# Regrouped projection steps and an rwkv stage that opens with its pair products

## The reference

```
def rwkv7_branch(p, mu, w0, w_up, a0, a_up, g_up, k_k, k_a, r_k, gn_g, gn_b):   # first block
    p = p + (token_shift(p) - p) * mu
    r, k, v, wd, ad, gd = _split(p, (A_WIDTH, A_WIDTH, A_WIDTH, A_RANK_W, A_RANK_A, A_RANK_G))
    w_log = -jax.nn.softplus(-(w0 + jnp.tanh(wd) @ w_up).astype(F32)) - 0.5
    decay = jnp.exp(-jnp.exp(w_log))
    a = jax.nn.sigmoid((a0 + ad @ a_up).astype(F32))
    g = jax.nn.sigmoid(gd) @ g_up
    kk = hd(k * k_k)
    kk = kk * lax.rsqrt(jnp.maximum(jnp.sum(kk * kk, axis=-1, keepdims=True), 1e-24))
    k_mod = hd(k.astype(F32) * (1.0 + (a - 1.0) * k_a.astype(F32)))
    y = rwkv7_scan(r_h, hd(decay), k_mod, v_h, -kk, kk * a_h)
    ...
def chunk_gated_delta_rule(q, k, v, g, beta):                                    # second block
    m = jnp.where(strict, jnp.einsum('bnhid,bnhjd->bnhij', k_beta, k) * decay_mat, 0.0)
    t_inv = lax.linalg.triangular_solve(eye + m, jnp.broadcast_to(eye, m.shape),
                                        left_side=True, lower=True, unit_diagonal=True)
    ...
```

## Time and profile before

| | |
|---|---|
| timed runs, median | 3095.12 us (3090.31 to 3096.48) |
| the profiled execution | 3103.75 us, its span 3100.7 us |
| mean granted TensorE clock | 0.925 |
| PE busy | 2743.8 us, 88% |
| DVE busy | 1880.1 us, 61% |
| ACT busy | 1342.8 us, 43% |
| DMA queue of the weights | 34.7% of 16 engines |

### The profile page before, as it was taken

How to read it: one execution, slowest core, us unless ns; L and a number is a source line. 1 busy time by engine, 2 the same in 40 slices (tenths; PEclk the granted TensorE clock), 3 DMA queues, 4 the chain that set the end, 5 groups by cost and what they waited for, 6 DMA issues and landing times. The chain is left out here.

```text
span 3100.7 us, 58400 instructions
## 1 busy us (share of the span) xinstructions
PE 2743.8 (88%) x25404; PEld 2336.9 (75%) x25404; DVE 1880.1 (61%) x2644; ACT 1342.8 (43%) x1882; POOL 87.9 (3%) x120
## 2 busy tenths in 40 slices
PE   7887778999887688999998888889999988978899
PEld 6776656888776657898887775678888877757788
DVE  5755766975765766956656444656565655446564
ACT  5413334655413244645453232544454532325453
POOL 0020000000110000000000200000000011000000
PEclk9897889999997889999998888989999988889999
DMA  5211114564211123554542121335655421113353
GB/s 222 96 43 55 69 56 149 192 214 174 83 59 52 69 96 136 203 196 165 203 152 103 42 71 40 112 138 201 221 179 203 151 77 56 69 41 130 143 199 128
DMA packets 54686, 386.48 MB, mean 125 GB/s; under 512 B 6688, under 2 KB 7328, under 8 KB 8352
## 3 DMA queue, kind: packets, MB, share of 16 engines
q1 hardware_dynamic: 54432, 382.76, 34.7%
HBM read 381.69 MB, written 1.05 MB: 123 GB/s over the span
## 5 line engine op out<-in xcount | busy, mean ns | idle before, releaser
L321 PE MATMUL banks<-normed_high,weights_high 128*128 128x256 f16 (+1 forms) x4096 | 1141.6, 279 | 42.7 <-DVE weights_low L307 20.1
L322 PE MATMUL banks<-normed_low,weights_high 128*128 128x256 f16 (+1 forms) x4096 | 1140.2, 278 | 0.0
L323 PE MATMUL banks<-normed_high,weights_low 128*128 128x256 f16 (+1 forms) x4096 | 1139.7, 278 | 0.0
L307 DVE SCALAR_TENSOR_TENSOR weights_low<-weight_ring,weights_high 128x2048 f16<-128x2048 f32 x334 | 761.2, 2279 | 406.3 <-ACT weights_high L301 391.9
L301 ACT ACTIVATE weights_high<-weight_ring 128x2048 f16<-128x2048 f32 x306 | 580.2, 1898 | 274.8 <-PE banks L323 262.6
L321 PE MATMUL banks<-projected,weights_high 128*128 128x256 f16 x1696 | 472.3, 278 | 72.4 <-DVE projected L332 72.4
L321 PEld LDWEIGHTS banks<-normed_high,weights_high 128*128 128x128 f16 (+1 forms) x4096 | 409.7, 100 | 121.7 <-issue 30.2
L322 PE MATMUL banks<-projected,weights_high 128*128 128x256 f16 x1696 | 472.7, 279 | 0.0
L323 PE MATMUL banks<-projected,weights_low 128*128 128x256 f16 x1696 | 472.2, 278 | 0.0
L323 PEld LDWEIGHTS banks<-normed_high,weights_low 128*128 128x128 f16 (+1 forms) x4096 | 408.5, 100 | 55.8
L322 PEld LDWEIGHTS banks<-normed_low,weights_high 128*128 128x128 f16 (+1 forms) x4096 | 408.6, 100 | 55.5 <-issue 1.3
(11 more groups left out here) (398 smaller groups left out, 3021.2 us busy)
## 6 DMA issues: line engine op xcount, KB each, us to landing
weight_ring<-w SPq DMA_DIRECT2D x356, 1024.0 KB, 4.8
small_weights<-small SPq DMA_DIRECT2D x2, 1280.0 KB, 7.3
constants<-const SPq DMA_DIRECT2D x1, 1601.0 KB, 10.1
weight_ring<-w SPq DMA_DIRECT2D x2, 640.0 KB, 3.8
residual<-xt SPq DMA_DIRECT2D x1, 1024.0 KB, 4.8
small_weights<-small SPq DMA_DIRECT2D x2, 512.0 KB, 10.4
out<-residual SPq DMA_DIRECT2D x4, 256.0 KB, 2.5
parameters<-par SPq DMA_DIRECT2D x2, 115.5 KB, 9.4
```

Of the source, the lines that this page charges most:

```text
L307: nc.vector.scalar_tensor_tensor(out=self.part(self.mem.w_low, g), in0=self.part(self.mem.ring, g), scalar=W_SCALE, in1=self.part(self.mem ...
L321: pe.matmul(out, w_high, high, start=start, stop=False, skip_group_check=skip)
L322: pe.matmul(out, w_high, low, start=False, stop=False, skip_group_check=skip)
L323: return pe.matmul(out, w_low, high, start=False, stop=stop, skip_group_check=skip)
```

## The change

1. *Token shift.* ScalarE copies each of the first 14 tiles twice: `raw`, as it is, and the tile scaled by (1 - mu). VectorE adds mu times the raw tile shifted by one token, two tiles behind each `low` from job 3 to job 9. The subtraction over all 14 tiles and the block of 14 shifts are gone.
2. *Order of the rwkv steps.* The keys' sum moves from group 10 to 6, their root ahead of tanh and sigmoid, their spread from group 14 to 11, the bonus product from 15 to 13, the near operands in front of the end; the copies of the far operands go to ScalarE.
3. *High and low parts.* The highs of the two jobs past the stage are made within the loop, and in the first block the low of the first of them at the end of the stage instead of at the start of the rwkv stage.
4. *rwkv stage.* It opens with the pair products. The transposes of v stand behind solver level 1 of the first chunk, those of the two operands behind level 3; ScalarE copies them out. The filler tiles 0 and 1 stand behind the pair products.
5. *Second block.* Roots of the unit norms, transposes of the columns and of v and the spreads stand behind groups 11 and 12; two copies go to ScalarE.

```diff
+            if i == 0 and beside.keep is not None:
+                need("mu_kept", 1)
             for n, (g, c0, m, part, tile) in enumerate(grp):
...
+                got, scale = mem.ps[part:part + m, i % BANKS, n * T:(n + 1) * T], PART_X
+                if beside.keep is not None and tile < 14:
+                    nc.scalar.activation(beside.raw[:, tile, :], got, ACT.Copy, scale=PART_X)
+                    scale = beside.keep[:, tile:tile + 1]
+                ins = nc.scalar.activation(mem.proj[part:part + m, tile, :], got, ACT.Copy,
+                                           scale=scale)
             ins.then_inc(sig("bank_free"), 1)
-            while split_up_to < jobs[-1] and used[split_up_to + 1 - RING] <= i + 1:
+            while (split_up_to < jobs[-1] + ahead and
+                   used[split_up_to + 1 - RING] <= i + 1):
                 split_up_to += 1
                 stream.high(act, nc, sig, split_up_to)
...
-        self.vector = {9: [self.shift_low_rank], 10: [self.shift], 11: [self.keys_squared],
...
-        self.scalar = {7: [self.low_rank_in], 9: [self.gates_of_a], 12: [self.exps],
-                       13: [self.keys_root], "end": []}
-        self.tensor = {8: [self.low_rank_up], 10: [self.keys_sum], 14: [self.keys_spread],
-                       15: [self.bonus_sum], "end": []}
+        self.vector = {"begin": [self.mu_kept],
+                       3: [self.shift(0)], 4: [self.shift(2)], 5: [self.shift(4)],
...
+                       14: [self.keys_unit], 15: [self.bonus_values], 16: [self.operands_near],
+                       "end": [self.operands_far, self.operands_state]}
+        self.scalar = {7: [self.keys_root, self.low_rank_in], 8: [self.gates_of_a],
+                       11: [self.exps], 15: [self.operands_copied], "end": []}
+        self.tensor = {6: [self.keys_sum], 8: [self.low_rank_up], 11: [self.keys_spread],
+                       13: [self.bonus_sum], "end": []}
...
+            solver.scalar(act, nc, sig, 0, {1: [values_by_token], 3: [high(3), keys_by_token]})
...
+                if n == 0:
+                    need("near_seen", 1)
+                    fill.tensor(pe, sig, 0)
+                else:
+                    need("mt_ready", 2)
                 fill.tensor(pe, sig, (1, 4)[n])
...
-                              else {"growth": [lambda pe: need("fill_out", 2)]})
+                              else {"growth": [lambda pe: need("fill_out", 2)],
+                                    1: [turn_values], 3: [turn_keys]})
...
-        self.tensor = {5: [self.beta_spread], 11: [self.units_sum],
-                       "end": [self.spread_q, self.spread_k, self.gate_spread, self.turn_v,
-                               self.turn_k]}
+        self.tensor = {5: [self.beta_spread],
+                       11: [self.units_sum, self.turn_columns, self.turn_v],
+                       12: [self.spread_q, self.spread_k],
+                       "end": [self.turn_k, self.gate_spread]}
...
+    def shift(self, first):
+
+        def step(link, say, need):
+            need("bank_free", first // 2 + 1)
+            for i in (first, first + 1):
+                p = self.mem.proj[:, i, 1:T]
+                say(self.nc.vector.scalar_tensor_tensor(out=p, in0=self.raw[:, i, 0:T - 1],
+                                                        scalar=self.col("mu", i), in1=p,
+                                                        op0=ALU.mult, op1=ALU.add), "shifted")
```

More of the change, by code:

```diff
@@ L466, in arrived, with project_stage @@
             pe.wait_ge(self.sig("u_low"), at.index(k) + 1)
-def project_stage(nc, mem, sig, stream, groups, first, gain, ready, spare, loaded, beside, ahead):
+def project_stage(nc, mem, sig, stream, groups, first, gain, ready, spare, loaded, beside, ahead,
+                  lows_ahead=0):
     norm = Norm(mem, Cutter(mem.scratch), sig, gain, ready, *spare)
@@ L492, in vector @@
         loaded(dve)
+        for step in beside.vector.get("begin", ()):
+            step(link, say, need)
         for n, g in enumerate(jobs[2:]):
@@ L498, in vector @@
             step(link, say, need)
+        for n in range(lows_ahead):
+            stream.low(dve, nc, sig, jobs[-1] + 1 + n, len(jobs) + n)
     def scalar(act):
@@ L563, with __init__ @@
 class Filler:
-    def __init__(self, mem, stream, tiles, banks, ahead):
+    def __init__(self, mem, stream, tiles, banks, ahead, lows_ahead=0):
         self.mem, self.stream = mem, stream
         self.tiles, self.banks, self.ahead = tiles, banks, ahead
+        self.lows_ahead = lows_ahead
         self.jobs = sorted({t[0] for t in tiles})
@@ L574, in sync @@
     def sync(self, sp, sig):
-        self.stream.load_behind(sp, sig, self.jobs[0], len(self.jobs))
+        st = self.stream
+        for n, g in enumerate(self.jobs):
+            if n >= self.lows_ahead:
+                sp.wait_ge(sig("lows"), n + 1 - self.lows_ahead)
+            if g + RING < len(st.jobs):
+                st.load(sp, g + RING)
     def high(self, act, nc, sig, n):
@@ L1516, in _ @@
             beside[1][6] = [low(5)]
-            low(0)()
-            need("turned", 1)
-            say(V.tensor_copy(p_v, two(4)), "by_token")
-            say(V.tensor_copy(bh_t, ps[:, 6, :]), "by_token")
-            say(V.tensor_copy(kh_t, ps[:, 7, :]), "by_token")
             for n in range(NBLK):
@@ L1584, in _, with values_by_token, keys_by_token @@
             out(1)
-            solver.scalar(act, nc, sig, 0, {3: [high(3)]})
+            def values_by_token():
+                need("values_turned", 1)
+                say(A(p_v, two(6), ACT.Copy), "by_token")
+            def keys_by_token():
+                need("keys_turned", 1)
+                say(A(bh_t, ps[:, 6, :], ACT.Copy), "by_token")
+                say(A(kh_t, ps[:, 7, :], ACT.Copy), "by_token")
+            solver.scalar(act, nc, sig, 0, {1: [values_by_token], 3: [high(3), keys_by_token]})
             out(2, 3)
@@ L2586, in spread_q @@
     def spread_q(self, pe, need):
+        need("columns", 1)
         need("unit_inverses", 1)
@@ L2973, in mixers1 @@
             rwkv_stage(nc, mem, sig, rwkv,
-                       Filler(mem, stream, later_tiles_1(mem, at[layer]), RWKV_BANKS, AHEAD))
+                       Filler(mem, stream, later_tiles_1(mem, at[layer]), RWKV_BANKS, AHEAD, 1))
             gates_at = at[layer] + GATES_AT1
```

143 lines of the change are left out of this document (74 added, 69 removed).

## The result

The changed kernel took 3069.66 us (median of 4 runs, 3068.65 to 3071.81) against 3095.8 (3090.31 to 3102.78); ratio 0.9908, 95% interval 0.9892 to 0.9925. 3066 had been forecast. The profiled execution took 3070.36 us with a span of 3068.4 and a mean clock of 0.929 (before: 3103.75, 3100.7 and 0.925): 33.4 us less in this pair, 26.1 less in the medians.

What follows compares the result with a forecast made beforehand. TensorE, busy 88% of 3100.7 us, bounds the kernel, with gaps where mixers are prepared and solved. A -19.4, B -5.0, C -5.8 sum to -30.2: 3064.9 on the median, said as 3066; range 3059 to 3073, 8 in 10 3052 to 3082.

Steps and rivals of the forecast that it cites:

- A: Rwkv project stage, both layers of the first block: regrouped steps end it 9.7 us earlier a layer, 19.4 in all.
- VectorE's tail: End of the rwkv project stage: 15.0 us of VectorE work behind the bonus product, hidden by 1.4 us.
- B: Rwkv stage, both layers of the first block: pairs first, transposes within the solver; -2.5 us a layer, between -0.5 and -3.9.
- Pairs start at once: -6.7 us: Front of the rwkv stage: the first pair product no longer stands 6.7 us into the stage.
- 12.7 us from first pair to first add: Front of the rwkv stage: first solver add 12.7 us behind the first pair instead of 9.9, filler 0 now between.
- The solver's +1.4: Rwkv stage's solver: turned tiles and ScalarE's copies cost 1.4 us a layer, with half clock 3.2.
- C: Delta preparation, both layers of the second block: a gain of 2.9 us a layer, bounds +0.5 to -4.5.
- both layers 5.8: Delta preparation: the 2.9 us gain read in one layer, taken for both as 5.8 us.
- rival 4: First chunk's solver, both rwkv layers: transposes let the clock fall to 1.2 GHz, 42 us lost, 3107 us; chance 0.04.
- Rival 2: Clock helps: delta stage's opening gains 2.9 us a layer, rwkv stages open at full clock, 1 us less each; 3058, chance 0.14.
- The sum: Whole kernel: the three parts' gains add to -30.2 us, 3073.6 on the profiled execution, 3064.9 on the median.

Runs made afterwards that it cites:

- b_undone: The changed kernel with the rwkv stage of before: transposes and filler 0 at its head, their copies on VectorE; 3071.63 us, ratio 0.9921.
- the kernel with C undone: The changed kernel with the second block's preparation as before; 3071.32 us, ratio 0.992.

## Why the prediction was right, and where it was not

**A, forecast -9.7 a layer.** Measured at the stages' starts, the second against the same low parts late in the first layer: -10.0 and -11.4. The stage was forecast to start at 136.9 and started at 136.64; group, keys' sum, half-clock up-products, spread and the border came as priced, and VectorE's tail was hidden by about half a us, where 1.4 had been forecast (its two low parts were summed as 2.21 us each, and they take 2.29). In the second layer TensorE waited 0.87 us and not 2.3: ScalarE found the root's table loaded, so two loads stood there instead of three. ScalarE's timeline, the root in the first layer and in the second:

```profile
76.11 1.28 ACT L1436 ACT_TABLE_LOAD   x1
...
748.38 0.21 ACT L1436 ACTIVATE scratch<-scratch 128x16 f32<-128x16 f32 x1
748.61 1.28 ACT L1420 ACT_TABLE_LOAD   x1
```

**B, forecast -2.5 a layer.** The direction held, the term failed at the step "Pairs start at once: -6.7 us". Those 6.7 us had been read in a trace in which TensorE came to the transposes from 7.5 us of idling, at 1.2 GHz; A took that idling away, and the low part from the stage's head, and with A in place the same work is 4.7 us. The part was priced against the kernel before and not against the kernel with the other part in it. The next step, 12.7 us from first pair to first add, came out as 12.75 in the second layer and 14.4 in the first, where 48 filler products took 7.07 us and not 5.3. The solver's +1.4 is +1.41. In all 0.4 a layer at full clock, just outside the forecast's own bounds of 0.5 and 3.9.

**C, forecast -2.9 a layer.** -2.8 in the first, -1.0 in the second. The step at fault is the doubling, "both layers 5.8": the term was read in one layer of the kernel before, with its groups at 0.86, and in the other they ran at 1.00. The step itself was sized rightly, since the kernel with C undone took 28.1 and 28.0 us there and the changed one 25.3 in both. That the clock would help the delta stage's opening did not come: it ran at 0.50 behind a wait of 2.97 us as it had behind 4.84.

**The clock.** With eight transposes behind level 1 and eight behind level 3 the solver's window ran at 1.00, and so it did without them (b_undone, its two layers below): transposes did not bring the clock down there, and rival 4 did not come. The Trainium skill, "TensorE: Matmul & The Clock Gate", section "Part 4: PE-mode transpose", says that transposes do not count as busy time in the same way. The solver says little on this, since its eight transposes last 1.1 us among other products; what does not agree are the 16 transposes of the kernel before, behind which the clock was at 0.97.

```profile
151.10:174.90 23.80, 18.83 (x516) 17.27 (x517) 16.24 (x32) 4.58 (x13) 5.81 (x7) 1.00 0.30 96
823.60:847.40 23.80, 18.87 (x516) 17.30 (x517) 16.26 (x31) 4.58 (x13) 5.76 (x7) 1.00 0.30 99
```

Rival 2 came in part: the first layer's pair products took 3.91 us, at full clock, but the second's 5.54, and the delta stage's opening stayed at 0.50. Over 43 executions the kernel before follows its mean clock, from 3104.7 us at 0.923 to 3091.1 at 0.929. At 0.929 the changed kernel takes 3070.0 (mean of 6 executions). So 21 of the 26 us are there at equal clock, and 5 come with the clock's rise from 0.927, the median of before. The two cannot be parted cleanly: in the padded kernel no order was changed and only waits were added, and the mean clock fell to 0.924.

**The sum.** -30.2 was meant for the profiled pair, which gave -33.4, and for the medians, which gave -26.1. The profiled execution of before, 8 us above its median, was one with much half clock; that part was no more to be gained on the median. The 3066 on the median was 4 us too low; the 1.1 us by which it stands above the sum's 3064.9 have no term behind them. That it came so near is partly luck: by the traces A was 2.0 us too small (-21.4 for -19.4), B 4.1 too large (-0.9 at full clock for -5.0), and C 1.9 too large (-3.9 for -5.8).

## What to carry to other kernels

Price a part against the kernel that has the other parts in it: work that ran at half clock behind a wait is cheaper once the wait is gone, and it is the part that takes the wait away that earns this. Where TensorE waits often, count a removed wait at more than its length (here 1.6 times, in two kernels), and judge an edit of 2 us in the timed runs, not in one trace, in which slow stretches of 3 to 10 us come and go. Before an engine's result that TensorE waits for, look for table loads and small operations that nobody needs yet: moving one root was worth 4 us. Before a term is doubled for a second layer, read that layer's rows too: here the same code took 28.09 us in one and 26.36 in the other.

## What the runs showed of the hardware that was not expected

- 8.2 us of useless work on VectorE, with 14.0 us of waits for TensorE in two places, cost 22.3 us, and TensorE's same products took 10 us longer in the trace. The clock in the 60 us behind the waits was 0.91 and 0.90; in three traces without the padding it was 0.97, 0.91 and 0.97 in the first layer and 0.94, 0.97 and 0.94 in the second.
- The same 24 up-products took 4.89, 7.51, 8.19 or 9.30 us behind the same wait of 2.29 us in different executions and kernels; behind 0.76 to 0.87 us they took 4.89 in 17 cases of 17.
- Sixteen transposes took half as long each (0.11 us start to start) behind 1.67 us of idling as behind 7.56 (0.21).
